# Transposed probabilities as the moving operand in the first mixers of a two-block decoder, with the gate carrying the softmax division

## What is computed

```python
h = rmsnorm(x, norm_g)
a_u, a_v, a_z, b_b, b_c, b_x, b_z, c_q, c_k, c_v, c_z, d_q, d_k, d_v, d_z = split(h @ w_in)
y_a = silu(layernorm(conv31(a_u * sigmoid(a_v)) + conv_b)) * silu(a_z)
y_b = b_b * conv3(b_c * b_x) * silu(b_z)
y_c = window_attention(rope(c_q), rope(c_k), c_v, sink) * silu(c_z)   # "C", 4 query heads, 2 key heads
y_d = neighbourhood_attention(d_q, d_k, d_v, rpb) * silu(d_z)         # "D", 4 heads
x = x + concat(y_a, y_b, y_c, y_d) @ w_out
```

## Time and profile before

| | us |
|---|---|
| runs shown, median (lowest to highest), 3 runs | 1252.49 (1251.99 to 1252.55) |
| the profiled execution, its own time | 1250.78 |
| its span, first to last instruction | 1249.0 |
| TensorE busy | 1232.9 |
| VectorE busy | 869.5 |
| ScalarE busy | 685.3 |
| GpSimd busy | 159.3 |

### The profile page before, as it was taken

The page is one execution under the profiler, slowest core; times in us unless marked ns, Lnnn a source line. Parts: engine busy times, 40 slices in busy tenths (PEclk is TensorE's granted clock), DMA queues, the critical chain, the costliest instruction groups (busy, mean ns, idle before and its releaser), DMA issues.

```text
span 1249.0 us, 24135 instructions
## 1 busy us (share of the span) xinstructions
PE 1232.9 (99%) x10072; PEld 1162.4 (93%) x10072; DVE 869.5 (70%) x1372; ACT 685.3 (55%) x1100; POOL 159.3 (13%) x210
## 2 busy tenths in 40 slices
PE   9999999999999999999999999999999999999997
PEld 7889878999999988799999999999998879999997
DVE  6988798878665567767666556667546676767742
ACT  7674666555554465556554544555447546555542
POOL 4102500375001110012000010000120002100001
PEclk9999999999999999999999999999999999999999
DMA  9535644556655654335555555555555433655551
GB/s 330 181 117 184 229 140 130 178 177 207 199 193 184 198 173 149 118 119 189 200 188 201 186 186 203 203 192 188 194 170 186 136 119 122 216 190 185 188 198 34
DMA packets 61388, 221.09 MB, mean 177 GB/s; under 512 B 7264, under 2 KB 7392, under 8 KB 61024
## 3 DMA queue, kind: packets, MB, share of 16 engines
q1 hardware_dynamic: 60768, 218.87, 53.1%
q0 software_dynamic: 224, 0.53, 0.2%
q10 hardware_dynamic: 288, 0.16, 0.1%
HBM read 218.48 MB, written 1.05 MB: 176 GB/s over the span
## 4 chain that ended last, share of the span: by engine, by line
PE 91%; DVE 5%; ACT 2%; issue 1%; POOL 1%; DMA 0%; POOLq 0%; DVEq 0%; ACTq 0%
PE pb L476 13%; PE pb L477 13%; PE pb L478 13%; PE pb L491 8%; PE pb L493 8%; PE pb L492 8%; PE pb L456 7%; PE pb L458 6%; PE pb L457 6%; PE pb L549 3%; DVE s_wl L1236 2%; DVE s_acc L1388 2%; PE pb L578 1%; PE pb L602 1%; ACT s_at_s L945 1%
## 5 line engine op out<-in xcount | busy, mean ns | idle before, releaser
L1236 DVE TENSOR_TENSOR s_wl<-s_wraw,s_wh 128x1024 fp32r<-128x1024 f32 (+1 forms) x411 | 504.1, 1247 | 137.5 <-ACT s_wh L877 136.8
L877 ACT ACTIVATE s_wh<-s_wraw 128x1024 fp32r<-128x1024 f32 (+1 forms) x411 | 421.2, 1048 | 182.5 <-PE pb L478 82.9
L476 PE MATMUL pb<-s_xh,s_wh 128*128 128x256 f32 x1296 | 359.1, 277 | 0.0
L478 PE MATMUL pb<-s_xh,s_wl 128*128 128x256 f32 x1296 | 358.3, 276 | 0.0
L477 PE MATMUL pb<-s_xl,s_wh 128*128 128x256 f32 x1296 | 358.3, 276 | 0.0
L477 PEld LDWEIGHTS pb<-s_xl,s_wh 128*128 128x128 f32 x1296 | 243.5, 188 | 0.0
L476 PEld LDWEIGHTS pb<-s_xh,s_wh 128*128 128x128 f32 x1296 | 243.5, 188 | 0.0
L478 PEld LDWEIGHTS pb<-s_xh,s_wl 128*128 128x128 f32 x1296 | 243.4, 188 | 0.0
L456 PE MATMUL pb<-s_wh,s_xh 128*128 128x512 f32 x448 | 181.0, 404 | 1.1 <-DVE s_wl L1236 1.1
L491 PE MATMUL pb<-s_hh,s_wh 128*128 128x256 f32 x660 | 182.2, 276 | 0.0
L492 PE MATMUL pb<-s_hl,s_wh 128*128 128x256 f32 x660 | 182.2, 276 | 0.0
(11 more groups left out here) (313 smaller groups left out, 1593.3 us busy)
## 6 DMA issues: line engine op xcount, KB each, us to landing
s_wraw<-in_w SPq DMA_DIRECT2D x407, 512.0 KB, 4.1
s_nab<-in_rpb SPq DMA_DIRECT2D x2, 1024.0 KB, 9.2
s_x<-in_x SPq DMA_DIRECT2D x4, 256.0 KB, 5.4
out_dram<-s_at_s SPq DMA_DIRECT2D x4, 256.0 KB, 2.7
s_cst<-in_cst SPq DMA_DIRECT2D x1, 680.0 KB, 8.9
s_wraw<-in_w SPq DMA_DIRECT2D x2, 256.0 KB, 4.5
s_ln<-in_lng POOLq DMA_DIRECT2D x2, 128.0 KB, 7.4
s_ln<-in_lnb POOLq DMA_DIRECT2D x2, 128.0 KB, 8.1
```

The source lines that it names most:

```text
L476: pe.matmul(o, wh[:, s, w], xk[0], start=k == v == 0, stop=False, skip_group_check=True)
L478: r = pe.matmul(o, wl[:, s, w], xk[0], start=False, stop=k == 7, skip_group_check=True)
L877: return act.activation(o, src, ACT.Copy, scale=scale)
L1236: dve.tensor_tensor(wl[:, s, part], wraw[:, r, part], wh[:, s, part].bitcast(F32), ALU.subtract).then_inc(low_done, 1)
```

## The change

In the first mixers the values become the loaded operand and the turned probabilities the moving one, as `weigh_turned` has it already; one function `weigh` now serves all four attentions, and its result comes out turned. The division by the denominator moves into the gate: `gated` multiplies silu(z) in place by the reciprocals, TensorE turns the gate instead of the result ("zC", "zD"), ScalarE copies it to SBUF and VectorE multiplies it with the attention's result (`product`) and takes the low half (`product_low`). `at1` keeps six turned slots instead of two and both attentions four slots of statistics. TensorE's small pieces of the two attentions stand at six places between tiles (28, 33, 36, 39, 42, 46) instead of ten, and the turn of the rotated queries and keys of layer 1 stands at tile 23 instead of 22. In the second mixers no operation changes, but pieces of L move one tile earlier and pieces on VectorE and ScalarE one unit earlier; `normalise(n, "L", 1)` now stands ahead of `split(n, 32)`. The diff at its core:

```diff
 class Attention:
-            self.stat = sb(name + "_stat", [P, 2, 4, 4], F32, where)
+            self.stat = sb(name + "_stat", [P, 4, 4, 4], F32, where)
-    co = sb("co", [P, 2, 256], F32, arena)
+    zc = sb("zc", [P, 512], F32, arena)
-    do = sb("do", [P, 2, 256], F32, arena)
+    zd = sb("zd", [P, 512], F32, arena)
-    at1 = Attention(arena, "at1", 2)
+    at1 = Attention(arena, "at1", 6)
...
     def turned_slot(a, t, kt):
-        return 2 if a in "FL" and t == 0 else kt
+        if a == "C":
+            return 2 + 2 * t + kt
+        if a == "D":
+            return kt
+        return 2 if t == 0 else kt
+
+    def stat_slot(a, t):
+        return 2 * t + (1 if a in "DL" else 0)
...
-        def weigh(n, a, t, value):
...
-            for h in range(4):
-                for kt in range(kts):
-                    r = pe.matmul(o[:, 64 * h:64 * (h + 1)], at_of(a).pt[:, kt, h, :], value(kt, h), start=kt == 0,
-                                  stop=kt == kts - 1)
-        def weigh_turned(n, a, value):
+        def weigh(n, a, value, ts=(0, 1), done=None):
+            kts = [keys_of(a, t) // P for t in range(2)]
...
-            for t in range(2):
+            for t in ts:
                 for p in range(2):
-                    for kt in range(t + 1):
+                    for kt in range(kts[t]):
                         for e in range(2):
                             h = 2 * p + e
                             r = pe.matmul(o[64 * e:64 * (e + 1), TOKENS * p + P * t:TOKENS * p + P * (t + 1)], value(kt, h),
...
 mixers1, TensorE:
-            tiles(n, 22)
+            tiles(n, 23 if l else 22)
...
-            tiles(n, 27)
+            tiles(n, 28)
             score_c(0)
-            tiles(n, 28)
             score_d(0)
-            tiles(n, 31 if l else 32)
+            tiles(n, 33)
             turn_weights(n, "C", 0)
-            tiles(n, 34 if l else 35)
-            weigh(n, "C", 0, value_c)
             score_c(1)
-            tiles(n, 36 if l else 37)
+            tiles(n, 36)
             turn_weights(n, "D", 0)
-            tiles(n, 38 if l else 39)
+            score_d(1)
+            tiles(n, 39)
+            turn_weights(n, "C", 1)
+            tiles(n, 42)
+            turn_weights(n, "D", 1)
+            weigh(n, "C", value_c)
             pe.wait_ge(dv_done, 2 * l + 2)
-            weigh(n, "D", 0, value_d)
-            score_d(1)
-            turn_weights(n, "C", 1)
-            tiles(n, 40 if l else 41)
-            weigh(n, "C", 1, value_c)
-            turn_weights(n, "D", 1)
-            tiles(n, 42 if l else 43)
-            weigh(n, "D", 1, value_d)
-            tiles(n, 44 if l else 45)
-            pe.wait_ge(gate_c_done, 2 * l + 2)
-            turn_block(n, "yC", lambda t, p: co[:, t, P * p:P * (p + 1)])
-            tiles(n, 48 if l else 50)
-            pe.wait_ge(gate_d_done, 2 * l + 2)
-            turn_block(n, "yD", lambda t, p: do[:, t, P * p:P * (p + 1)])
+            weigh(n, "D", value_d, (0,), (weighed_d0, 1))
+            tiles(n, 46)
+            weigh(n, "D", value_d, (1,))
+            for j, a in enumerate("CD"):
+                pe.wait_ge(gate_done[a], 2 * l + 2)
+                turn_block(n, "z" + a, lambda t, p: cdz[:, t, 256 * j + P * p:256 * j + P * (p + 1)])
...
 mixers1, ScalarE:
+            act.wait_ge(weighed_d0, l + 1)
+            turned_weights(n, "D", 1, 0, None)
+            turned_weights(n, "D", 1, 1, None)
             split(n, 26)
...
-            y_high(n, "yC", y1, 4)
+            split(n, 27)
+            for a, z in (("C", zc), ("D", zd)):
+                act.wait_ge(*full(n, "z" + a))
+                copy(z[:, :], psum(n, "z" + a)[:, :]).then_inc(*empty(n, "z" + a))
+            for a, z, k in (("C", zc, 4), ("D", zd, 6)):
+                act.wait_ge(*gone(n, "y" + a))
+                copy(flat(y1[0][:, k:k + 2, :]), z[:, :]).then_inc(yh_done, 1)
...
 mixers1, VectorE:
-            def gated(o, name, j, done):
+            def gated(a, j):
                 for t in range(2):
                     dve.wait_ge(*gone(n, ("in", 4, t)))
+                    dve.wait_ge(rec_s[a], 2 * l + t + 1)
+                    z = cdz[:, t, 256 * j:256 * (j + 1)].rearrange("p (h d) -> p h d", h=4)
+                    dve.tensor_tensor(z, z, at1.stat[:, stat_slot(a, t), 3, :].unsqueeze(2).to_broadcast([P, 4, 64]),
+                                      ALU.mult).then_inc(gate_done[a], 1)
...
+            def product(a, z):
+                dve.wait_ge(*gone(n, "z" + a))
+                dve.wait_ge(*full(n, "y" + a))
+                dve.tensor_tensor(z[:, :], z[:, :], psum(n, "y" + a)[:, :], ALU.mult).then_inc(*empty(n, "y" + a))
...
-            weighed(n, "C", 0, co)
             low_c(1, "tC01")
...
             conv(29 if l else 26)
-            y_low(n, "yC", y1, 4)
-            gated(do, "D", 1, gate_d_done)
+            product("C", zc)
+            product("D", zd)
             conv(30 if l else 27)
+            product_low("C", zc, 4)
+            product_low("D", zd, 6)
             split(n, 27)
...
 mixers2, TensorE:
-            tiles(n, 45)
+            tiles(n, 44)
             turn_block(n, "lq", lambda t, p: dlqk[:, t, P * p:P * (p + 1)])
-            tiles(n, 48)
+            tiles(n, 47)
             score_dil(0)
-            tiles(n, 51)
+            tiles(n, 50)
             turn_weights(n, "L", 0)
...
 mixers2, VectorE:
-            split(n, 31)
+            split(n, 30)
             turned_weights("L", 0, "yF")
             low_dil(1)
             advance(6)
             blocks(6)
+            normalise(n, "L", 1)
             split(n, 32)
-            normalise(n, "L", 1)
             turned_weights("L", 1, "yF")
```

More of the change, by code:

```diff
@@ L125 @@
 MISC = {
-    "b1": ("sum", "gate", "cq", "ck", "dq", "dk", "sC0a", "sC0b", "sD0a", "sD0b", "tC00", "tC01", "vC0", "sC1a", "sC1b",
-           "tD00", "tD01", "vD0", "sD1a", "sD1b", "tC10", "tC11", "vC1", "tD10", "tD11", "vD1", "yC", "yD", "conv",
-           "bx", "yA", "bz"),
+    "b1": ("sum", "gate", "cq", "ck", "dq", "dk", "sC0a", "sC0b", "sD0a", "sD0b", "tC00", "tC01", "sC1a", "sC1b",
+           "tD00", "tD01", "sD1a", "sD1b", "tC10", "tC11", "tD10", "tD11", "yC", "yD", "zC", "zD", "conv", "bx", "yA", "bz"),
     "f": ("sum", "rbc"),
@@ L341, in program @@
     ya_done, cv_done, dv_done, rope_done = sem("ya_done"), sem("cv_done"), sem("dv_done"), sem("rope_done")
-    yh_done, gate_c_done, gate_d_done = sem("yh_done"), sem("gate_c_done"), sem("gate_d_done")
+    yh_done, weighed_d0 = sem("yh_done"), sem("weighed_d0")
+    gate_done = {a: sem("gate_done" + a) for a in "CD"}
+    y_done = {a: sem("y_done" + a) for a in "CD"}
     bcx_done, bconv_done, bsilu_done, yb_done = sem("bcx_done"), sem("bconv_done"), sem("bsilu_done"), sem("yb_done")
@@ L516, in out_of_mixers @@
                     pe.wait_ge(yb_done, l + 1)
+                elif kind == "b1" and ks[0] == 0:
+                    pe.wait_ge(*gone(n, "yA"))
                 elif kind == "b1":
-                    pe.wait_ge(*gone(n, {0: "yA", 4: "yC", 6: "yD"}[ks[0]]))
+                    pe.wait_ge(y_done["C" if ks[0] == 4 else "D"], l + 1)
                 else:
@@ L616, in weigh_turned @@
                             r = pe.matmul(o[64 * e:64 * (e + 1), TOKENS * p + P * t:TOKENS * p + P * (t + 1)], value(kt, h),
-                                          at_of(a).pt[:, turned_slot(a, t, kt), h, :], start=kt == 0, stop=kt == t,
+                                          at_of(a).pt[:, turned_slot(a, t, kt), h, :], start=kt == 0, stop=kt == kts[t] - 1,
                                           skip_group_check=True)
-            r.then_inc(*fill(n, "y" + a))
+            r.then_inc(*(done or fill(n, "y" + a)))
         def turn_block(n, name, src, count=2):
@@ L1017, in mixers1 @@
             exponential(n, "C", 1)
-            turned_weights(n, "D", 0, 0, "vC0")
-            turned_weights(n, "D", 0, 1, "vC0")
             split(n, 23)
-            turned_weights(n, "C", 1, 0, "vD0")
-            turned_weights(n, "C", 1, 1, "vD0")
+            turned_weights(n, "D", 0, 0, None)
+            turned_weights(n, "D", 0, 1, None)
+            split(n, 24)
             exponential(n, "D", 1)
-            split(n, 24)
-            turned_weights(n, "D", 1, 0, "vC1")
-            turned_weights(n, "D", 1, 1, "vC1")
+            turned_weights(n, "C", 1, 0, None)
+            turned_weights(n, "C", 1, 1, None)
             split(n, 25)
@@ L1048, in mixers1 @@
                 copy(bcx[:, t, :], psum(n, ("in", 5, t))[:, 0:256], r(t)).then_inc(bcx_done, 1)
-            if not l:
-                y_high(n, "yD", y1, 6)
             split(n, 30 if l else 31)
@@ L1532, in mixers1 @@
                 split(n, 25)
-                gated(co, "C", 0, gate_c_done)
-                weighed(n, "D", 1, do)
+                gated("C", 0)
+                gated("D", 1)
                 conv(28)
```

80 lines of the change are left out of this document (28 added, 52 removed).

## The result

The changed kernel takes 1243.26 us (median of 4 runs, 1242.35 to 1245.81) where the kernel before takes 1252.26 on the same chip: a ratio of 0.9931, 95% interval 0.9914 to 0.9949, so 6 to 11 us faster, 9.0 by the medians. The forecast was 1243.2, and the profiled span fell from 1249.0 to 1240.5. The total is right to a tenth of a microsecond. Two of its terms are not, and they nearly cancel, as the stretches show.

The account below looks back on a forecast made before the run. TensorE, busy 1232.9 of 1249.0 us, was taken as the bound. Gains of 1.8 (layer 0), -0.6 (layer 1) and 8.1 us (second mixers), together 9.3, took 1252.49 to 1243.2 us, range 1236.0 to 1248.0.

Parts of the forecast that it names:

- Products and joints, 3.5 us a layer: First mixers, TensorE: cheaper product records give 3.35 us a layer, fewer slow stream starts behind groups 0.15.
- Rival (d): Products of C and D don't run in pairs: 6.7 us less gain, 1249.9 us; chance 0.03.
- Old waits of the first mixers: TensorE regains waits: rotated queries 1.1 us and C block 0 0.75 (layer 1), gated convolution 0.6 (layer 0).
- The wait for banks: New TensorE wait at D block 1's scores for banks VectorE empties: 2.3 us lost in layer 0, 3.0 in layer 1.
- I take one fall, 1.5 us: Clock drops to half behind one of the two bank waits, put in layer 1: 1.5 us, bounds none and two.
- The convolution's wait, layer 1: TensorE waits before the convolution's turn at tile 49, VectorE doing two products first: 1.45 us lost, between 0.5 and 2.
- Second mixers, 8.1 us: Wait for the normalisation goes in both second mixers, with its clock fall: twice 4.06 us, margin 1.4 us.
- The sum: Layer 0 gains 1.8 us, layer 1 -0.6, second mixers 8.1: together 9.3 us.
- (a): Bank waits at D block 1 don't arise, VectorE being there in time: 1236.4 us; chance 0.10.
- (b): Second mixers' wait shrinks but some 2 us of each stays, without a clock fall: 1247.2 us; chance 0.12.
- (c): VectorE runs late beside GpSimd, costing both mixers: 1256.9 us at 3 us late, slower than before; chance 0.05.
- (e): Gain is given back since weights then arrive too late: 1252 us; chance 0.05.

Follow-up runs that it names:

- one_half: The changed kernel with both heads of a pair's products written to the same 64 columns of the array; profiled span 1254.3 us, 13.8 more.
- taps_first: The changed kernel with layer 1's last two convolution taps ahead of the two products on VectorE; 1242.9 us, ratio 0.9935 to the kernel before.
- score_late: The changed kernel with the scores of D block 1 two tiles later on TensorE, at tile 38; 1237.6 us against 1250.7 for the kernel before.
- first_only: The changed kernel with the second mixers ordered as before; 1253.1 us against 1250.7 for the kernel before, ratio 1.0015.
- second_exact: The kernel before with all of the change's second-mixer edits and none of the first's; 1244.1 us against 1252.0, ratio 0.9940.
- unpaired: The changed kernel with products of all even heads first, then the odd, in all mixers; 1248.8 us against 1252.0 for the kernel before.

## Why the prediction was right, and where not

**Products and joints, 3.5 us a layer: mis-sized, 3.0.** Rows 6 gave 7.1 us for 128 records, and the changed kernel's 4.3 + 3.9 = 8.2 us against 15.2 gives 7.0. What was off is the edges. I summed the groups with scores, turns and products of each layer, from the stream's last start ahead of a group to its next, less the 0.23 us of a stream matmul in each and with the slower one behind: 16.5 us before in ten groups, 13.5 in six without their waits. That is 3.0 a layer. Rival (d), no pairing, is out: records of C and D take 61 to 67 ns in the changed kernel and 116 to 120 where one_half takes the pairing away. What the Trainium skill says (TensorE: Matmul & The Clock Gate, Part 3, "The mechanism"), that a weight load overlaps a running matmul only with another row group, does not hold here as it reads: products on all 128 rows ran two at a time when their columns differed.

**Old waits of the first mixers: right.** Rotated queries, layer 1: 1.96 - 0.80 = 1.16 us regained against 1.1. C block 0, layer 1: 1.83 - 1.02 = 0.81 against 0.75. The gated convolution, layer 0: 1.57 - 0.91 = 0.66 against 0.6. The first of them rests on one trace, though: in the old order the wait for the rotated queries was 0.94, 1.21 and 2.01 us in three traces, and in the changed order it came back once with 0.42 (taps_first).

**The wait for banks: right in place, releaser and size** (2.06 and 2.51 of idling against 2.0 and 2.8; in layer 0 both engines came 0.4 to 0.5 us later than in the walk, which cancels), and score_late shows the cause by taking it away. Over the seven traces it was 1.8 to 2.1 in layer 0 and 1.6 to 2.6 in layer 1.

**"I take one fall, 1.5 us": the step that failed.** It read from two waits with a fall (2.38, 2.39) and one without (0.94) that length decides, and put the fall into layer 1. The trace had it in layer 0, the seven traces have 0.86 falls a wait, counting the double one as two, and one costs 1.6 us. So the two waits bring 2.7 us on average over these traces, not 1.5. Over the executions it may be less: the changed kernel's granted clocks (0.996 on average, as in its trace with one fall) put it nearer to one. The same holds for the waits that went from the second mixers: both fell in the trace of before, one of two in that of first_only. The bounds given, none and two, hold all traces but the one with the double fall.

**The convolution's wait, layer 1: right** (1.38 us of idling; 1.59 lost against 1.45), and taps_first shows the cause.

**Second mixers, 8.1 us: right,** 8.2 in the trace and 7.9 by the medians of second_exact, with a margin on VectorE of 1.2 us (1.4 forecast).

**The sum.** Layer 0: 3.0 + 0.66 - 2.2 (the wait and its overlap) - 1.6 (fall) - 0.1 (a longer joint at the norm) = -0.3, as the stretch shows. Layer 1: 3.0 + 1.16 + 0.81 - 2.7 - 1.6 = 0.7, and it shows 0.8. That the total agreed to 0.1 us is luck within some 3 us of clock falls: the trace has 8.5 for a forecast 9.3. The other rivals: (a) no bank waits, is out, since both were there in every trace of that form; (b), a smaller wait in the second mixers, and (c), VectorE late by 2.4 us or more, did not occur; (e), the gain given back later, is out, as the feed-forward stretches kept their length.

## What to carry over

A rewrite that cuts an engine's work is worth what the new order of its groups leaves of it: here 6 us of saved work went nearly all into three places where TensorE came 1.4 to 2.5 us too early for another engine, and moving two groups by a tile or two and two taps by one place gave another 7 to 8 us, nearly as much as the whole change. Walk the list of the engine that empties the banks up to the point where they are claimed, and put the claim behind it. Price a wait of about 2 us on TensorE at its idle time plus most of a clock fall, as a chance and not as a rule, and compare medians of many executions where such waits stand.

## What was not expected

- Of 19 waits of 1.6 to 2.6 us in the mixers 14 were followed by half clock; 2.51 and 2.39 once were not, 1.78 was, and once the half clock lasted twice as long (0.51 over 187.2 to 194.0).
- Products of one half of the columns run beside those of the other even where they are issued in blocks: 61 ns a record against 109 alone, in unpaired. A product of D starts 0.32 us ahead of one of C that stands before it in the program.
- Waits and falls that are priced one by one don't add: the first mixers' edits gain 1 us beside those of the second mixers and lose 2 without them.
